# RWKV-7 scan on one core: where the N masks, the 16-row substitution and its buffers stand

## The chip, the cores and the metric

One core of one Trainium2 chip runs one program. The time is that of the device, in microseconds, for the whole program. The profile is one execution of it, with the instructions of TensorE (PE), its weight loads (PEld), VectorE (DVE), ScalarE (ACT), GpSimd (POOL) and the DMA issues of SyncE (SP).

## The reference, cut to what matters

Two transformer blocks are computed for 1024 tokens of width 1024 in float32. The first has two mixers side by side, an RWKV-7 mixer and a gated linear attention, and a feed-forward part; the second has neighbourhood attention, a convolution and a multilayer perceptron. The change touches the RWKV-7 scan alone, which has 8 heads of 64 channels and runs once forward and once backward:

```
def step(S, inp):
    r_t, w_t, k_t, v_t, kk_t, b_t = inp
    sa = jnp.einsum('bhij,bhj->bhi', S, -kk_t)
    S = (S * w_t[:, :, None, :] + sa[..., None] * b_t[:, :, None, :]
         + v_t[..., None] * k_t[:, :, None, :])
    return S, jnp.einsum('bhij,bhj->bhi', S, r_t)
y = (rwkv7_scan(r_h, heads(decay[:, :, 0]), k_h, v_h, kk, b_h, False)
     + rwkv7_scan(r_h, heads(decay[:, :, 1]), k_h, v_h, kk, b_h, True))
```

Everything ahead of the scan makes r, k, v, kk, b and the decays; what follows normalises y, multiplies by a gate and projects.

## The kernel before

Each engine has its own program, written out by hand in `rwkv_scan_pe`, `rwkv_scan_dve`, `rwkv_scan_act`, `rwkv_scan_pool` and `rwkv_scan_sp`. Engines meet through counters: `.then_inc(*dve.one("nm", n, d))` marks a point, and `wait_ge(dve["nm", n, d])` waits for it. An engine does its instructions in the order in which they are written, so that a wait holds all that stands behind it. `dve.c` makes VectorE wait for its own last instruction first.

The scan is done in 16 chunks (`NSUB`) of 64 tokens. The 16 pairs of head and direction lie as 8 lanes, 4 for each direction `d`, with two heads one above the other in the 128 partitions. Inside a chunk the recurrence is a triangular system, whose matrix has to be inverted. For a chunk n the steps are:

- `products(n)`, VectorE, lines 1697 to 1702: the factor F, four wide multiplies that make AR (three homes) and BK (one home), and a copy of the last decay. It waits for the exponentials, for the outputs of chunk n-3, and for the transposes of chunk n-1 (`pe["tr", n - 1, 1]`), which read BK.
- TensorE, gram products `gb` and `gk` (line 1480, names s_AR and s_BK): the products of BK with AR, in PSUM. VectorE multiplies them by the triangular masks at line 1716: `gb` gives NM (the N masks, counter `nm`), `gk` gives MM (the M masks, counter `mm`).
- TensorE, transposes of BK (line 1555, counter `tr`), which write to the same PSUM bank as `gb` and so wait for `nm`. ScalarE copies them out as BKT (line 1623).
- The diagonal 16x16 blocks of NM go by DMA to DRAM (line 1446) and come back as 16 small loads (line 1423) onto 32 partitions in `N16`: ten issued by SyncE, six by GpSimd. GpSimd writes the identity to `Z16` (line 1638), and `substitute_dve` inverts the blocks there in 15 steps of two dependent small instructions (lines 1662 and 1663), with a transposed copy at the end (line 1665, counter `x16`).
- The inverse goes to DRAM (line 1455) and back in 8 loads (line 1432, `inverse_back`) into ZZ, four by SyncE and four by GpSimd.
- Two levels join the 16-row blocks to 32 and to 64 rows: TensorE `p4`, VectorE mask `t4` (line 1736), TensorE `l4` (lines 1578, 1579), VectorE `zz` (line 1740), then `p5`, `t5` (line 1744), `l5`, and `xt` (line 1750), which gives XT, the whole inverse.
- With the state: right sides `rh`, ScalarE Rn, TensorE `uu` with XT, ScalarE U, TensorE `ss`, VectorE state sum (line 1711) and scaling by F (line 1721), TensorE outputs `yy`, taken to B by ScalarE in the first half (line 1619) and added there by VectorE in the second (line 1727).

The loop runs over u from -2 to 15. A pass u works on three chunks at once: the state of chunk u, the levels of chunk m = u + 1, and the masks and the substitution of chunk n = u + 2; it also makes the products of chunk u + 3. TensorE's order in a pass is: gb, gk (n), uu, ss, yy (u), tr (n), in every second pass the sums of the log decays (line 1489), rh (m), p4, l4, p5, l5 (m). VectorE's order is: state sum (u), N and M masks (n), state scaling, output sums (u, second half), products (u + 3), t4, zz, t5 (m), substitution steps 0 to 3 (n), xt (m), substitution steps 4 to 14 and the copy (n). gb of a pass waits for t5 and gk for xt of the pass before. In pass 14 four multiplies for a later stage (line 1910) stand ahead of t4.

SyncE's order per chunk n (`rwkv_scan_sp`) is: wait for the N masks of n, N out; wait for the inverse of n - 1 to be in DRAM, its four loads; wait for N to be out, ten block loads; in every second chunk the load of the decays (line 1441); wait for `x16` of n, inverse out. N out and the block loads count on one counter, `t_n`. GpSimd's order is: inverse loads of n - 1, identity of n, block loads of n.

Of the kernel before, what the change touches and what calls it, by code (L numbers as in the profile page):

```python
# [10 lines left out]
ALU = mybir.AluOpType  # L11
ACTF = mybir.ActivationFunctionType
# [13 lines left out]
NSUB = 16  # L26
# [150 lines left out]
def rep(ap, n):  # L177
    return ap.unsqueeze(1).to_broadcast([ap.shape[0], n] + list(ap.shape[1:]))
# [29 lines left out]
class Kernel:  # L208
    def __init__(self, nc, ins, out):
# [12 lines left out]
        self.t_lat = [self.transfer(f"t_lat{k}") for k in range(2)]  # L222
        self.t_zb, self.t_nb = self.transfer("t_zb"), self.transfer("t_nb")
        self.t_x = [self.transfer(f"t_x{k}") for k in range(3)]
        self.t_a = [self.transfer(f"t_a{k}") for k in range(4)]
# [99 lines left out]
    def plan_block1(self):  # L325
# [76 lines left out]
        self.En, self.Eb = sb("s_En", [PART, LANES, 2, CH]), sb("s_Eb", [PART, LANES, 2, CH + 1])  # L402
        self.eye16, self.N16 = sb("eye16", [32, 2, 16, 16]), sb("s_N16", [32, 2, 16, 16])
        self.XT, self.S = ([sb(n, [PART, LANES, CH]) for k in range(2)] for n in ("s_XT", "s_S"))
# [1013 lines left out]
    def blocks_there(self, eng, counter, n, ks):  # L1418

        nd = self.dram["nd"]  # L1420
        for k in ks:
            for d in range(2):
                eng.e.dma_start(self.N16[4 * k:4 * k + 4, d], nd[n % 2, 4 * d:4 * d + 4, 16 * k:16 * k + 16, 16 * (k % 4):16 * (k % 4) + 16]) \
                    .then_inc(*counter.one("in", n))
# [10 lines left out]
    def rwkv_scan_sp(self):  # L1435
        sp, sg, pe, dve = self.sp, self.dram["sg"], self.pe, self.dve
        nd, zd = self.dram["nd"], self.dram["zd"]

        def sig(t):
            sp.wait_ge(pe["cum", t - 1, 1])  # L1440
            sp.e.dma_start(self.sig[:], sg[:, t].rearrange("d p c -> p d c")).then_inc(*self.t_in.one("sig", t))

        sig(1)
        for n in range(NSUB):
            sp.wait_ge(dve["nm", n, 1])
            sp.e.dma_start(nd[n % 2].rearrange("l p c -> p l c"), self.NM[n % 3][:, :, 0, :]).then_inc(*self.t_n.one("out", n))
            if n:
                sp.wait_ge(self.t_z["out", n - 1], self.pool["zero"])
                self.inverse_back(sp, self.t_z, n - 1, range(0, 8, 2))
            sp.wait_ge(self.t_n["out", n])  # L1450
            self.blocks_there(sp, self.t_n, n, range(0, 5))
            if n % 2 and (n + 3) // 2 < NBLK:
                sig((n + 3) // 2)
            sp.wait_ge(dve["x16", n])
            sp.e.dma_start(zd[n % 2].rearrange("k x d w i c -> (k x) (d w i c)"), self.Z16[:].rearrange("p d w i c -> p (d w i c)")) \
                .then_inc(*self.t_z.one("out", n))
        sp.wait_ge(self.t_z["out", NSUB - 1])
        self.inverse_back(sp, self.t_z, NSUB - 1, range(0, 8, 2))
        i = self.i
        sp.wait_ge(dve["pr", NSUB - 1])  # L1460
        for dst, src in ((self.r_hones[:], i["k_head_ones"]), (self.r_hsel2[:], i["k_head_sel"]), (self.r_gup[:], i["rwkv_g_up"][0]),
                         (self.r_sglo2[:], self.dram["lo"][2])):
            sp.e.dma_start(dst, src).then_inc(*self.t_misc.one("ro"))
        sp.e.dma_start(self.r_v[:], self.dram["v"]).then_inc(*self.t_keep.one("v_back"))
        self.meet(sp, "rwkv_scan", self.t_misc["ro"], self.t_keep["v_back"])
# [138 lines left out]
    def rwkv_scan_act(self):  # L1604
        pe, act, dve, ps = self.pe, self.act, self.dve, self.ps
        L = [slice(0, 4), slice(4, 8)]
        for u in range(-2, NSUB):
# [12 lines left out]
            if u + 2 < NSUB:  # L1620
                for d in range(2):
                    act.wait_ge(pe["tr", u + 2, d])
                    act.e.activation(self.BKT[(u + 2) % 3][:, L[d]].rearrange("p l w c -> p l (w c)"), self.fb(d, 0), ACTF.Copy) \
                        .then_inc(*act.one("BKT", u + 2, d))
            if u % 2 == 0 and (u + 4) // 2 < NBLK:
                self.exps_act((u + 4) // 2)
        self.meet(act, "rwkv_scan")

    def rwkv_scan_pool(self):
        pool = self.pool  # L1630
        pool.e.memset(self.S[0][:], 0.0).then_inc(*pool.one("zero"))
        for n in range(NSUB + 1):
            if n:
                pool.wait_ge(self.t_z["out", n - 1], pool["zero"])
                self.inverse_back(pool, self.t_zb, n - 1, range(1, 8, 2))
            if n < NSUB:
                pool.wait_ge(self.t_misc["r_const"])
                pool.e.tensor_copy(self.Z16[:, :, 1], self.eye16[:]).then_inc(*pool.one("one", n))
                pool.wait_ge(self.t_n["out", n])
                self.blocks_there(pool, self.t_nb, n, range(5, 8))  # L1640
        self.meet(self.pool, "rwkv_scan")

    def substitute_dve(self, n, first, end):
# [3 lines left out]
        if first == 0:  # L1647
            dve.wait_ge(self.pool["one", n])
            dve.wait_ge(self.t_n["in", n], self.t_nb["in", n])
        N, Z = self.N16[:, 0], self.Z16[:, 0, 1]  # L1650

# [15 lines left out]
    def rwkv_scan_dve(self):  # L1667
# [11 lines left out]
        def products(n):  # L1679
# [22 lines left out]
            dve.c.tensor_copy(lanes(self.last[:]), end).then_inc(*dve.one("pr", n))  # L1702

        products(0)
        for u in range(-2, NSUB):
            n, m = u + 2, u + 1
# [5 lines left out]
            if n < NSUB:  # L1712
                for w, to, name in ((0, self.NM[n % 3], "nm"), (1, self.MM[n % 3], "mm")):
                    for d in range(2):
                        dve.wait_ge(pe[("gb", "gk")[w], n, d])
                        dve.e.tensor_tensor(to[:, L[d]].rearrange("p l a b -> p l (a b)"), self.fb(d, w),
                                            rep(self.gram_mask[:, d].rearrange("p a b -> p (a b)"), 4), ALU.mult).then_inc(*dve.one(name, n, d))
            if u >= 0 and m < NSUB:
# [12 lines left out]
            if u + 3 < NSUB:  # L1731
                products(u + 3)
            if 0 <= m < NSUB:
                for d in range(2):
                    dve.wait_ge(pe["p4", m, d])
                    dve.e.tensor_tensor(self.T[:, L[d]], self.hb(d, 0), rep(self.lev_mask[:, 0, d], 4), ALU.mult).then_inc(*dve.one("t4", m, d))
            if 0 <= m < NSUB:
                for d in range(2):
# [6 lines left out]
            if n < NSUB:  # L1745
                self.substitute_dve(n, 0, 4)
            if 0 <= m < NSUB:
                for d in range(2):
                    dve.wait_ge(pe["l5", m, d])
                    dve.e.tensor_tensor(self.XT[m % 2][:, L[d]], self.ZZ2[:, L[d], 1], self.hb(d, 1), ALU.subtract).then_inc(*dve.one("xt", m, d))  # L1750
            if n < NSUB:
                self.substitute_dve(n, 4, 15)
        self.meet(dve, "rwkv_scan")
# [1488 lines left out]
```

## Time and profile before

| what | us |
|---|---|
| three runs: lowest, median, highest | 3499.68, 3499.96, 3500.47 |
| the profiled execution's own time | 3487.46 |
| its span | 3486.2 |
| the scan, from its first product on VectorE to its last inverse, in the span | 700 to 1076 |

Over the whole span TensorE is busy for 3188.2 us (91%), VectorE for 2211.3 (63%), ScalarE for 971.9 (28%) and GpSimd for 469.5 (13%). Times in rows are microseconds from the start of the span. A row of a timeline gives the start, the duration, the engine, the line of the program, what is written and read, the shapes and, in brackets, how long the engine had been idle and what ended that.

### The profile page before, as it was taken

What the parts mean: (1) busy time and instruction counts of PE and PEld (TensorE: products, weight loads), DVE (VectorE), ACT (ScalarE), POOL (GpSimd) and SP (SyncE); (2) the same over time, 40 slices, a digit from 0 to 9 for tenths busy, and PEclk for the clock granted to TensorE, in tenths of its full rate; (3) what the DMA queues carried; (4) which work ended last, traced back from release to release, by engine and by line L of the source; (5) the groups of instructions that cost most, each with busy time, mean ns of one, the idle gap of its engine ahead of it and who ended that gap; (6) DMA issues with size and microseconds to landing.
All of it is one profiled execution on the core that took longest, in us unless ns stands there. A gap on an engine that the chain in (4) does not pass through costs nothing.

```text
span 3486.2 us, 58522 instructions
## 1 busy us (share of the span) xinstructions
PE 3188.2 (91%) x25755; PEld 2622.4 (75%) x25755; DVE 2211.3 (63%) x2948; ACT 971.9 (28%) x1514; POOL 469.5 (13%) x373
## 2 busy tenths in 40 slices
PE   6988788979987999999999897998998799999996
PEld 4777767778885878888888676875667688888885
DVE  5758655778887444444444575997556566666666
ACT  4544233312113221111111444112663111111112
POOL 2530023423224000000000121000001011111110
PEclk9979788989998999999999998999999899999999
DMA  4410044322224011111111202114001111111111
GB/s 131 122 66 14 16 142 138 111 45 42 37 36 166 19 55 51 40 55 53 38 55 43 91 31 74 49 43 99 2 2 61 43 49 49 49 49 49 49 49 67
DMA packets 242726, 207.27 MB, mean 59 GB/s; under 512 B 66744, under 2 KB 205255, under 8 KB 241959
## 3 DMA queue, kind: packets, MB, share of 16 engines
q1 hardware_dynamic: 223527, 176.82, 17.1%
q10 hardware_dynamic: 13824, 25.17, 2.2%
q0 software_dynamic: 5120, 1.53, 0.5%
q8 instruction: 202, 3.31, 0.4%
q14 instruction: 53, 0.43, 0.0%
HBM read 171.93 MB, written 29.64 MB: 58 GB/s over the span
## 4 chain that ended last, share of the span: by engine, by line
PE 70%; DVE 17%; ACT 5%; POOL 2%; issue 2%; DMA 2%; SPq 1%; ACTq 0%; DVEq 0%; POOLq 0%
PE ps L2169 23%; PE ps L2184 17%; PE ps L2031 5%; PE ps L636 3%; PE ps L637 3%; PE ps L638 3%; DVE Yc L2794 2%; DVE s_tmp L1662 2%; DVE s_Z L1663 2%; PE ps L2893 2%; PE ps L2921 1%; PE ps L2911 1%; PE ps L1480 1%; POOL a_x L2544 1%; PE ps L1008 1%
## 5 line engine op out<-in xcount | busy, mean ns | idle before, releaser
L3198 DVE TENSOR_TENSOR H<-H,ps 128x1024 f32<-128x1024 f32 x256 | 312.7, 1221 | 181.6 <-PE ps L2184 174.8
L2334 DVE TENSOR_TENSOR fsum<-fsum,ps 128x1024 f32<-128x1024 f32 x168 | 205.2, 1221 | 312.4 <-PE ps L2184 310.3
L2184 PE MATMUL ps<-dh,hh 128*128 128x512 f32 x864 | 340.0, 393 | 19.9 <-DVE hl L2149 13.9
L2184 PE MATMUL ps<-dl,hh 128*128 128x512 f32 x864 | 338.7, 392 | 0.0
L2184 PE MATMUL ps<-dh,hl 128*128 128x512 f32 x864 | 338.6, 392 | 0.0
L2169 PE MATMUL ps<-hn_h,uh 128*128 128x512 f32 x704 | 275.8, 392 | 7.2 <-DVE ul L1779 4.7
L2169 PE MATMUL ps<-hn_l,uh 128*128 128x512 f32 x704 | 275.4, 391 | 0.0
L2169 PE MATMUL ps<-hn_h,ul 128*128 128x512 f32 x704 | 275.3, 391 | 0.0
L2169 PE MATMUL ps<-hx_h,uh 128*128 128x512 f32 x512 | 200.9, 392 | 8.4 <-DVE hx_l L2149 5.3
L2184 PEld LDWEIGHTS ps<-dh,hh 128*128 128x128 f32 x864 | 163.8, 190 | 58.0 <-DVE hl L2149 15.6
L2169 PE MATMUL ps<-hx_l,uh 128*128 128x512 f32 x512 | 200.4, 391 | 0.0
L2169 PE MATMUL ps<-hx_h,ul 128*128 128x512 f32 x512 | 200.4, 391 | 0.0
L2184 PEld LDWEIGHTS ps<-dh,hl 128*128 128x128 f32 x864 | 163.7, 189 | 34.4
L2184 PEld LDWEIGHTS ps<-dl,hh 128*128 128x128 f32 x864 | 163.7, 189 | 33.9
L2544 POOL TENSOR_TENSOR a_x<-a_x,a_t 128x512 f32<-128x512 f32 x84 | 129.0, 1535 | 338.0 <-ACT a_t L2533 335.5
L3168 POOL TENSOR_TENSOR dw<-dw,g_row 128x1024 f32<-128x1024 f32 x32 | 77.7, 2431 | 710.0 <-DMA dw<-in_w_mlp_dram 710.0
L2169 PEld LDWEIGHTS ps<-hn_h,uh 128*128 128x128 f32 x704 | 133.1, 189 | 35.5 <-DVE ul L1779 5.2
L2794 DVE SCALAR_TENSOR_TENSOR Yc<-cp,cols,Yc 128x1024 f32<-128x1024 f32 x120 | 154.2, 1285 | 4.3
L2169 PEld LDWEIGHTS ps<-hn_l,uh 128*128 128x128 f32 x704 | 133.2, 189 | 27.7
L2169 PEld LDWEIGHTS ps<-hn_h,ul 128*128 128x128 f32 x704 | 133.1, 189 | 27.8
L636 PE MATMUL ps<-hx_h,cw 128*128 128x512 f32 x320 | 130.8, 409 | 17.2 <-DVE cw L616 7.5
L3177 ACT ACTIVATE relu<-ps 128x1024 f32<-128x1024 f32 x32 | 32.9, 1029 | 404.9 <-PE ps L2169 404.9
(473 smaller groups left out, 7345.8 us busy)
## 6 DMA issues: line engine op xcount, KB each, us to landing
aw<-in_w_ada_dram ACTq DMA_DIRECT2D x96, 256.0 KB, 2.9
uw<-in_w_mlp_dram SPq DMA_DIRECT2D x32, 512.0 KB, 4.3
dw<-in_w_mlp_dram SPq DMA_DIRECT2D x32, 512.0 KB, 5.2
uw<-in_ffn_gate_dram SPq DMA_DIRECT2D x22, 512.0 KB, 4.0
uw<-in_ffn_up_dram SPq DMA_DIRECT2D x22, 512.0 KB, 5.3
dw<-in_ffn_down_dram SPq DMA_DIRECT2D x22, 512.0 KB, 5.9
cw<-in_w_in_dram SPq DMA_DIRECT2D x20, 512.0 KB, 3.8
o_w<-in_w_out_dram SPq DMA_DIRECT2D x16, 512.0 KB, 9.9
```

The costliest lines, as they stand in the source:

```text
L636: pe.e.matmul(ps[0:m, 2 * (j % 2) + h, :], wh[:, k, :], xh, start=(k == 0), stop=False)
L637: pe.e.matmul(ps[0:m, 2 * (j % 2) + h, :], wh[:, k, :], xl, start=False, stop=False)
L638: mm = pe.e.matmul(ps[0:m, 2 * (j % 2) + h, :], wl[:, k, :], xh, start=False, stop=(k == kc - 1))
L1662: dve.c.tensor_tensor(part, col, pivot, ALU.mult).then_inc(*dve.one())
L2031: mm = pe.e.matmul(self.ps[:, 2 * (t % 2) + hf, :], x[a](k), w[b](k)[:, half(hf)], start=(n == 0 and m == 0), stop=(n == len(order) - 1 an ...
L2169: mm = pe.e.matmul(ps[:, 2 * pair + h, :], w[:, col], x[h][v][:, k, :], start=(k == 0 and m == 0), stop=(k == DC - 1 and m == 2))
L2184: mm = pe.e.matmul(ps[:, 2 * pair + hf, :], v[s][:, blk(t)], w[:, half(hf)], start=(m == 0), stop=(m == 2))
L2334: return dve.c.tensor_tensor(f, f, new, ALU.add) if g else dve.c.tensor_copy(f, new)
L2544: pool.c.tensor_tensor(acc[:], acc[:], self.a_t[who][:], ALU.add).then_inc(*pool.one("ada", q, who))
L2794: dve.c.scalar_tensor_tensor(out=o, in0=x[:, w:w + TOK], scalar=self.col("dw", n + 4 * w), in1=o, op0=ALU.mult, op1=ALU.add) \
L3168: pool.e.tensor_tensor(w, w, self.g2_row[:], ALU.mult).then_inc(*pool.one("m", "dw", g))
L3198: return dve.c.tensor_tensor(h, h, self.ps[:, 4 + 2 * (t % 2):6 + 2 * (t % 2), :], ALU.add)
```

## The change

- The N masks of chunk n + 1 are made in the pass before: in pass u they stand behind `xt` and ahead of substitution step 9. The M masks stay where they were.
- The substitution of chunk n is cut otherwise: steps 0 to 6 stand ahead of the mask `t4`, step 7 behind it, step 8 behind `t5`, steps 9 to 14 behind the N masks of n + 1.
- `N16` has two homes, used in turn.
- SyncE's order per chunk becomes: N out, wait, ten block loads, and then wait for `x16` of the chunk before, inverse out, wait, its four loads. N out has a counter of its own, `t_no`.
- GpSimd does its six block loads ahead of its four inverse loads, and no longer writes the identity; ScalarE does (copy of 32x512), behind BKT of the chunk and once the inverse of the chunk before is in DRAM.

```diff
-        self.eye16, self.N16 = sb("eye16", [32, 2, 16, 16]), sb("s_N16", [32, 2, 16, 16])
+        self.eye16, self.N16 = sb("eye16", [32, 2, 16, 16]), [sb("s_N16", [32, 2, 16, 16]) for k in range(2)]
...
+        def back(n):
+            sp.wait_ge(dve["x16", n])
+            sp.e.dma_start(zd[n % 2].rearrange("k x d w i c -> (k x) (d w i c)"), self.Z16[:].rearrange("p d w i c -> p (d w i c)")) \
+                .then_inc(*self.t_z.one("out", n))
+            sp.wait_ge(self.t_z["out", n], self.pool["zero"])
+            self.inverse_back(sp, self.t_z, n, range(0, 8, 2))
...
         for n in range(NSUB):
             sp.wait_ge(dve["nm", n, 1])
-            sp.e.dma_start(nd[n % 2].rearrange("l p c -> p l c"), self.NM[n % 3][:, :, 0, :]).then_inc(*self.t_n.one("out", n))
+            sp.e.dma_start(nd[n % 2].rearrange("l p c -> p l c"), self.NM[n % 3][:, :, 0, :]).then_inc(*self.t_no.one("out", n))
+            sp.wait_ge(self.t_no["out", n])
+            self.blocks_there(sp, self.t_n, n, range(0, 5))
             if n:
-                sp.wait_ge(self.t_z["out", n - 1], self.pool["zero"])
-                self.inverse_back(sp, self.t_z, n - 1, range(0, 8, 2))
-            sp.wait_ge(self.t_n["out", n])
-            self.blocks_there(sp, self.t_n, n, range(0, 5))
+                back(n - 1)
...
+                act.wait_ge(self.t_z["out", u + 1] if u + 1 >= 0 else self.t_misc["r_const"])
+                act.e.activation(self.Z16[:, :, 1], self.eye16[:], ACTF.Copy).then_inc(*act.one("one", u + 2))
...
         for n in range(NSUB + 1):
+            if n < NSUB:
+                pool.wait_ge(self.t_no["out", n])
+                self.blocks_there(pool, self.t_nb, n, range(5, 8))
             if n:
                 pool.wait_ge(self.t_z["out", n - 1], pool["zero"])
                 self.inverse_back(pool, self.t_zb, n - 1, range(1, 8, 2))
-            if n < NSUB:
-                pool.wait_ge(self.t_misc["r_const"])
-                pool.e.tensor_copy(self.Z16[:, :, 1], self.eye16[:]).then_inc(*pool.one("one", n))
-                pool.wait_ge(self.t_n["out", n])
-                self.blocks_there(pool, self.t_nb, n, range(5, 8))
...
         products(0)
+        masked(0, 0)
...
             if n < NSUB:
-                for w, to, name in ((0, self.NM[n % 3], "nm"), (1, self.MM[n % 3], "mm")):
...
+                masked(1, n)
...
             if u + 3 < NSUB:
                 products(u + 3)
+            if n < NSUB:
+                self.substitute_dve(n, 0, 7)
...
+            if n < NSUB:
+                self.substitute_dve(n, 7, 8)
...
             if n < NSUB:
-                self.substitute_dve(n, 0, 4)
+                self.substitute_dve(n, 8, 9)
...
+            if n + 1 < NSUB:
+                masked(0, n + 1)
             if n < NSUB:
-                self.substitute_dve(n, 4, 15)
+                self.substitute_dve(n, 9, 15)
```

`masked(w, n)` holds the body of the old loop: for each direction it waits for `gb` or `gk` and multiplies by the triangular mask.

## Rows read from the trace of the kernel before

**Rows 1.** Busy time by stretch, in the scan: stretch, length, then each engine, granted clock.
```profile
800.00:900.00 100.00, 91.66 (x2465) 86.26 (x2463) 80.93 (x236) 20.74 (x52) 29.40 (x49) 1.00 0.22 38
1000.00:1060.00 60.00, 50.39 (x1434) 47.28 (x1432) 46.70 (x140) 7.00 (x16) 17.31 (x29) 1.00 0.17 25
```

**Rows 2.** Timeline of VectorE: start of the first level mask in three passes.
```profile
734.49 0.89 DVE L1736 TENSOR_TENSOR s_T<-ps,lev_mask 128x256 f32<-128x256 f32 x2 [0.61 <-PE ps L1480]
...
1048.21 0.89 DVE L1736 TENSOR_TENSOR s_T<-ps,lev_mask 128x256 f32<-128x256 f32 x2 [3.94 <-PE ps L1480]
...
1069.88 0.42 DVE L1736 TENSOR_TENSOR s_T<-ps,lev_mask 128x256 f32<-128x256 f32 x1 [0.56 <-PE ps L1480]
```

**Rows 3.** Chain of waits in one pass: start, duration, engine or DMA, what.
```profile
882.05 0.60 DVE s_Z L1665
...
883.31 1.21 DVE s_NM L1716 x2
884.54 0.38 SPq L1446
...
886.73 3.61 DMA s_ZZ<-zd_dram
```

**Rows 4.** Timeline of VectorE, two steady passes, from one level mask to the next.
```profile
868.39 0.89 DVE L1736 TENSOR_TENSOR s_T<-ps,lev_mask 128x256 f32<-128x256 f32 x2 [1.20 <-PE ps L1480]
870.10 0.69 DVE L1740 TENSOR_TENSOR s_ZZ<-s_ZZ,ps 128x512 f32<-128x512 f32 x1 [0.82 <-PE ps L1579]
...
873.08 0.20 DVE L1662 TENSOR_TENSOR s_tmp<-s_N,s_Z 32x30 f32<-32x30 f32 x1
...
875.00 0.73 DVE L1750 TENSOR_TENSOR s_XT<-s_ZZ,ps 128x256 f32<-128x256 f32 x2
...
877.59 0.28 DVE L1662 TENSOR_TENSOR s_tmp<-s_N,s_Z 32x128 f32<-32x128 f32 x1
...
886.51 0.17 DVE L1697 TENSOR_TENSOR s_F<-s_last,s_Eb 128x8 f32<-128x8 f32 x1
886.60 0.68 DVE L1698 TENSOR_TENSOR s_AR<-r_kk,s_Eb 128x512 f32<-128x512 f32 x1
887.20 1.12 DVE L1699 TENSOR_TENSOR s_BK<-r_bb,s_En 128x512 f32<-128x512 f32 x1
...
891.12 0.89 DVE L1736 TENSOR_TENSOR s_T<-ps,lev_mask 128x256 f32<-128x256 f32 x2 [1.37 <-PE ps L1480]
```

**Rows 5.** Timeline of VectorE, first pass (u = -2): products of chunk 1.
```profile
710.80 0.17 DVE L1697 TENSOR_TENSOR s_F<-s_last,s_Eb 128x8 f32<-128x8 f32 x1 [1.17 <-PE ps L1555]
```

**Rows 6.** Timeline of ScalarE, first pass: the second direction of BKT.
```profile
710.80 0.60 ACT L1623 ACTIVATE s_BKT<-ps 128x512 f32<-128x512 f32 x1 [0.25 <-PE ps L1555]
```

**Rows 7.** Timeline of TensorE, one steady pass: gram products, uu, transposes.
```profile
873.50 3.91 PE L1480 MATMUL ps<-s_AR,s_BK 64*64 64x128 f32 x64
877.25 1.10 PE L1480 MATMUL ps<-s_Rn,s_XT 64*64 64x64 f32 x32
...
883.97 2.08 PE L1555 MATMUL ps<-eye,s_BK 64*64 64x64 f32 x64 [0.56 <-DVE s_NM L1716]
```

**Rows 8.** Waits from 740 to 1040 us: total, times, longest.
```profile
PEld ps L1480 <- DVE s_XT L1750: 3.7, 14, 0.3
```

**Rows 9.** Timeline of GpSimd, the steady pass: the identity's copy.
```profile
887.14 0.62 POOL L1638 COPY s_Z<-eye 32x512 f32<-32x512 f32 x1
```

**Rows 10.** Timeline of SyncE's queue, first passes and second to last.
```profile
707.91 0.38 SPq L1446 DMA_DIRECT2D nd_dram<-s_NM  x1
710.50 3.57 SPq L1423 DMA_DIRECT2D s_N<-nd_dram  x10
726.15 0.32 SPq L1455 DMA_DIRECT2D zd_dram<-s_Z  x1
...
1062.45 0.32 SPq L1455 DMA_DIRECT2D zd_dram<-s_Z  x1
```

**Rows 11.** Timeline of VectorE, pass 14: the four multiplies for the later stage.
```profile
1064.46 4.87 DVE L1910 SCALAR_TENSOR_TENSOR r_rkv<-r_rkv,cols 128x1024 f32<-128x1024 f32 x4
```

More of the change, by code:

```diff
@@ L223, in __init__ @@
         self.t_zb, self.t_nb = self.transfer("t_zb"), self.transfer("t_nb")
+        self.t_no = self.transfer("t_no")
         self.t_x = [self.transfer(f"t_x{k}") for k in range(3)]
@@ L1422, in blocks_there @@
             for d in range(2):
-                eng.e.dma_start(self.N16[4 * k:4 * k + 4, d], nd[n % 2, 4 * d:4 * d + 4, 16 * k:16 * k + 16, 16 * (k % 4):16 * (k % 4) + 16]) \
+                eng.e.dma_start(self.N16[n % 2][4 * k:4 * k + 4, d], nd[n % 2, 4 * d:4 * d + 4, 16 * k:16 * k + 16, 16 * (k % 4):16 * (k % 4) + 16]) \
                     .then_inc(*counter.one("in", n))
@@ L1445, in rwkv_scan_sp @@
             sp.wait_ge(dve["nm", n, 1])
-            sp.e.dma_start(nd[n % 2].rearrange("l p c -> p l c"), self.NM[n % 3][:, :, 0, :]).then_inc(*self.t_n.one("out", n))
+            sp.e.dma_start(nd[n % 2].rearrange("l p c -> p l c"), self.NM[n % 3][:, :, 0, :]).then_inc(*self.t_no.one("out", n))
+            sp.wait_ge(self.t_no["out", n])
+            self.blocks_there(sp, self.t_n, n, range(0, 5))
             if n:
-                sp.wait_ge(self.t_z["out", n - 1], self.pool["zero"])
-                self.inverse_back(sp, self.t_z, n - 1, range(0, 8, 2))
-            sp.wait_ge(self.t_n["out", n])
-            self.blocks_there(sp, self.t_n, n, range(0, 5))
+                back(n - 1)
             if n % 2 and (n + 3) // 2 < NBLK:
                 sig((n + 3) // 2)
[L1454 to L1458, printed above, removed]
+        back(NSUB - 1)
         i = self.i
@@ L1647, in substitute_dve @@
         if first == 0:
-            dve.wait_ge(self.pool["one", n])
+            dve.wait_ge(self.act["one", n])
             dve.wait_ge(self.t_n["in", n], self.t_nb["in", n])
-        N, Z = self.N16[:, 0], self.Z16[:, 0, 1]
+        N, Z = self.N16[n % 2][:, 0], self.Z16[:, 0, 1]
         def both(x, second, first, rest):
@@ L1702, in products, with masked @@
             dve.c.tensor_copy(lanes(self.last[:]), end).then_inc(*dve.one("pr", n))
+        def masked(w, n):
+            to, name = ((self.NM[n % 3], "nm"), (self.MM[n % 3], "mm"))[w]
+            for d in range(2):
+                dve.wait_ge(pe[("gb", "gk")[w], n, d])
+                dve.e.tensor_tensor(to[:, L[d]].rearrange("p l a b -> p l (a b)"), self.fb(d, w),
+                                    rep(self.gram_mask[:, d].rearrange("p a b -> p (a b)"), 4), ALU.mult).then_inc(*dve.one(name, n, d))
         products(0)
+        masked(0, 0)
         for u in range(-2, NSUB):
@@ L1712, in rwkv_scan_dve @@
             if n < NSUB:
-                for w, to, name in ((0, self.NM[n % 3], "nm"), (1, self.MM[n % 3], "mm")):
[L1714 to L1717, printed above, removed]
+                masked(1, n)
             if u >= 0 and m < NSUB:
```

## The prediction

> **What bounds the kernel now.** I read the stretches first. In the RWKV scan neither engine is full all the time: in the middle of it TensorE is busy for 91.7 of 100 us and VectorE for 80.9, at a granted clock of 1.00, the upper of its two levels [rows 1]. So the scan is bound by a chain that goes round once per pass (one pass per chunk of 64 tokens, 16 chunks). The start of the first level mask of each pass gives the beat: from 734.49 to 1048.21 us there are 14 passes, 313.7 us, 22.4 us each [rows 2].
>
> The chain of waits shows the round: the substitution and its copy end on VectorE, VectorE does the state sum and the N masks, SyncE's queue (held by its wait for the N masks) only then issues the return of the inverse blocks, they land 3.6 us after the last issue, TensorE multiplies, and VectorE masks the level [rows 3]. VectorE stood idle 1.37 us ahead of that mask [rows 4]. That idle time is what a substitution begun earlier could fill.
>
> What the reader must see beside it is a second chain, hidden today. The line that starts the products of chunk u+3 waits for the transposes of chunk u+2, as they read the one BK buffer that the products overwrite. In the first pass that wait is bare: F begins at 710.80, after 1.17 us idle put down to the transposes (L1555), at the moment at which ScalarE begins to read the last of them [rows 5, 6]. In a steady pass the wait is covered: the transposes start at 883.97 and take some 2.05 us, so end at 886.0, and F begins at 886.51 [rows 4, 7].
>
> **The steady pass, worked out.** I call L the start of the gram products of the next chunk; TensorE does its work in a fixed order from there. In the pass shown L is 873.50 [rows 7]. From L to the end of the transposes TensorE has the gram products (3.9 us), the inverse's product, state, outputs and transposes: 886.0 - 873.5 = 12.5 us. Two waits in it go: the 0.56 us of the transposes for the N mask (the passes looked at have 0.55 or 0.56) [rows 7], because that mask is now made a pass earlier; and up to 0.3 us of the second gram product for XT (3.7 us in 14 passes, 0.26 each) [rows 8], because XT has two substitution steps ahead of it where it had four. So the transposes end at L + 11.7.
>
> VectorE meanwhile: XT to L + 0.9; the N masks, two, together 1.2 us [rows 3], the second not before the gram product of its direction is through, at about half of 3.9 us: end at L + 2.7; steps 9 to 14 of the substitution, from step 7's start at 877.59 to the copy at 882.05, 4.46 us, less two steps of 0.63: 3.2 us [rows 3, 4], so L + 5.9. Copy, state sum, M masks and state scaling take today, with the N masks between them, 882.05 to 886.51; less the N masks' 1.2 that is 3.3 us: L + 9.2. In the second half of the scan the output sums follow, which TensorE allows at about L + 9.6 (the transposes' 883.97 less their wait, and less 0.26): L + 10. The products can't start there, since the transposes end at L + 11.7. **So VectorE idles 1.5 to 2.5 us there**, where today it does not; the idle time has moved, not gone.
>
> After it come, in VectorE's own order, products and then seven substitution steps, all ahead of the level mask. Products: today from F at 886.51 to the mask at 891.12 less its idle 1.37, 3.2 us, in which one of the four wide multiplies took 1.12 us, beside GpSimd's copy of the identity from 887.14 on; another of them took 0.68 us [rows 4, 9]. That copy leaves GpSimd, so I take 3.2 less 0.4, 2.8 us (bounds 2.8 and 3.2). Seven steps: the first four 1.98 us (873.08 to the XT pair at 875.00 and on it by 0.06 us), the next three from that pair's end at 875.76 to 877.59, 1.83 us [rows 4]. With 0.15 us of hand-over the mask starts at L + 11.7 + 2.8 + 1.98 + 1.83 + 0.15 = L + 18.5.
>
> From the mask to the next L: 868.39 to 873.50, 5.1 us, all of it TensorE and VectorE in turns [rows 4, 7]. Step 7 (0.63 us) fits in the 0.82 us idle that VectorE has behind the masks, and step 8 stands behind the last mask where four steps stood. Nothing is won or lost there (bounds -0.1 and +0.3). The pass is 5.1 + 18.5 = **23.6 us against 22.4**, and in the 13 passes that have products +15.6 us.
>
> **The identity on ScalarE.** The trace has no such copy on ScalarE. From below it costs nothing; from above, ScalarE's 128x512 evacuation takes 0.60 us [rows 6], and at that price it ends at L + 12.9, behind the evacuation of the transposes (it waits for the inverse of the chunk before to have left Z16, too, at L + 11.6 with N's 2.6 us), 1.6 us ahead of the first step at L + 14.5. I take nothing; queued behind it are exponentials and right sides not needed before that. The Trainium skill (SBUF — State Buffer, "Who interferes with whom") says that only VectorE and GpSimd share a port pair, and that ScalarE has its own. The stretched multiply agrees for GpSimd, and no run here yet shows the identity written from ScalarE. By the rule the products take 2.8 us; were the stretch to move along to ScalarE, 3.2 us, and the sum 5.2 us more.
>
> **The queues.** SyncE now does per chunk: N out, wait, ten block loads into the other home, and only then the inverse out and back. N out to the first block load took 2.6 us (707.91 to 710.50), the ten loads 3.6 us [rows 10], so that the inverse leaves at L + 2.7 + 0.1 + 2.6 + 3.6 = L + 9.0, though it is ready at L + 6.5. From its issue to the mask there were 7.4 us where no N load stood between (1062.45 to 1069.88) [rows 2, 10], so the mask could start at L + 16.4. In a crowded queue, with 2.6 us to land as for N and then the chain's 6.2 us from the end of N's issue (884.54 + 0.38) to the mask at 891.12 [rows 3, 4], it is L + 17.8. Both are ahead of L + 18.5, so the delay is hidden, with 0.7 to 2.1 us to spare. The same cover takes GpSimd's six loads and the sigma load, and the second home, without which the loads would have to wait for the substitution. The first step's other inputs (blocks at L + 11, identity) are there as well.
>
> **The ends of the scan.** First pass: chunk 0's inverse leaves today at 726.15, behind the copy of 0.6 us and steps 9 to 14 of 3.2 [rows 10]. Now the N mask of chunk 1 stands before step 9, at about 722.4 to 723.7; N lands at 726.3, the ten loads end at 729.9, the inverse leaves at 730.0, 3.8 us later. With the 7.4 to 8.8 us from there to the mask (as above), it comes at about 738.1 instead of 734.49: +3.6 us (bounds +1.2, the mask's own time, and +5). Second to last pass: no products are left, the mask comes at L + 17.1 against L + 17.5: -0.4 us. Last: today 1048.21 to 1069.88, 21.7 us [rows 2]. Now XT ends 6.0 us behind the mask (5.1 + 0.9), with nine steps done and not four; steps 9 to 14 and the copy take 3.8, and no N and no loads are ahead of the inverse, so it leaves at +9.9 and would allow the mask at +17.3. VectorE has the last output sum before it, which TensorE allows at +12.2 (from the inverse's product at 877.25 to the end of the outputs at 883.4 are 6.2 us [rows 7]), and four bonus products, 4.87 us [rows 11]: +17.5. So some -4.1 us (bounds -5 and -2).
>
> **Sum:** +15.6 + 3.6 - 0.4 - 4.1 = +14.7 us. The profiled execution took 3487.5 us over a span of 3486.2, so it would become 3502.2; the median of the runs shown, 3499.96, lies 12.5 us above the profiled one, and the same difference on it gives **3515 us**. The rest of the kernel is untouched.
>
> **Rivals.**
> (a) Not slower: the transposes are not the last thing the products wait for. It decides if they end before L + 9.2. Then the mask waits for the inverse alone, at L + 16.4 to 17.8: a pass of 21.5 to 22.9, and with the ends -13 to +6 us, near 3496 us, within the measurement's reach of no change or a little under it. For it speaks the idle VectorE today; against it that TensorE's work up to there is 11.7 us without a wait. In the full form of it the inverse comes free of the queue too and TensorE alone sets the pass: 11.7, 1 us of the sums (they run in every second pass), 2 of right sides and 0.7 to the mask, so 20.5 us, -25 us, 3476 us.
> (b) The inverse comes later than the mask could start, as ten loads stand ahead of it and N lands in crowded queues. At 1 us beyond L + 18.5 it adds 13 us: 3528 us. For it speak the 3.6 us from the last issue to the landing [rows 3], behind only four returns and one N; against it the 0.7 to 2.1 us to spare.
> (c) The clock. A pass with longer idle stretches on TensorE might be granted less than 1.00. Busy 84% of the time (50.4 of 60 us) it still had 1.00 [rows 1]; the new pass has 91.7% x 22.4 / 23.6 = 87% in the middle. As an estimate, half the clock doubles TensorE's 20 us of a pass, so that one pass at it would cost some +20 us. The rows speak against it.
>
> **Chances.** Forecast 0.77; (a) 0.06 near no change and 0.05 in full; (b) 0.08; (c) 0.02; unseen, of either sign, 0.02. The range takes the forecast's own bounds (steady passes +11 to +21, start and end -2 to +3) and half of (b): 3505 to 3526. I take 0.2%, 7 us, as what can be told from no change: slower 0.85, same 0.09, faster 0.06.
>
> **What the profile after would show.** Right: pass 23.6 us from level mask to level mask; VectorE idle ahead of F, put down to L1555's transposes, 1.5 to 2.5 us a pass; no idle worth a name ahead of the level mask; transposes without a wait for the N mask; all four wide multiplies at 0.68; the inverse leaving 2 us or more behind its copy. Wrong: an idle ahead of the level mask that ends with TensorE behind a transfer (b), F following the scaling without a gap (a), or a granted clock under 1.00 in the middle of the scan (c).

## The result and the profile after

The changed kernel takes 3526.45 us in the median of 4 runs (3520.85 to 3528.37); the kernel before, run with it, 3499.82 us (3496.81 to 3500.47). The ratio is 1.0075, with a 95% interval of 1.0058 to 1.0093: **slower by 26.6 us**, with 20 to 33 us by the interval, where 15 were forecast. The range ended at 3526, half a microsecond short of the median. The profiled execution took 3520.85 us over a span of 3519.5, 33.4 us more than the one of before. That is more than the medians differ by, as the profiled execution of before was 12.4 us under its median and this one 5.6.

First the stretches of the scan, as in [rows 1]: stretch, length, busy time of each engine, then granted clock, DMA share and GB/s.

```profile
800.00:900.00 100.00, 87.00 (x2295) 83.97 (x2293) 74.66 (x224) 20.64 (x50) 24.55 (x41) 0.93 0.23 40
900.00:1000.00 100.00, 86.95 (x2226) 84.22 (x2224) 74.43 (x217) 18.22 (x44) 24.08 (x40) 0.90 0.21 37
```

TensorE is busy for 87% of the time, which is the very share that the prediction gave, but at a clock of 0.93 and 0.90, not 1.00. Next VectorE's timeline, the lines that answer to [rows 2] and [rows 4]: F (now line 1700) and the first level mask (now line 1745).

```profile
764.58 0.73 DVE L1745 TENSOR_TENSOR s_T<-ps,lev_mask 128x256 f32<-128x256 f32 x2
...
781.42 0.17 DVE L1700 TENSOR_TENSOR s_F<-s_last,s_Eb 128x8 f32<-128x8 f32 x1 [2.69 <-PE ps L1558]
781.51 0.68 DVE L1701 TENSOR_TENSOR s_AR<-r_kk,s_Eb 128x512 f32<-128x512 f32 x1
782.12 0.68 DVE L1702 TENSOR_TENSOR s_BK<-r_bb,s_En 128x512 f32<-128x512 f32 x1
...
790.00 0.42 DVE L1745 TENSOR_TENSOR s_T<-ps,lev_mask 128x256 f32<-128x256 f32 x1 [1.84 <-PE ps L1483]
...
808.38 0.17 DVE L1700 TENSOR_TENSOR s_F<-s_last,s_Eb 128x8 f32<-128x8 f32 x1 [2.55 <-PE ps L1558]
...
815.04 0.74 DVE L1745 TENSOR_TENSOR s_T<-ps,lev_mask 128x256 f32<-128x256 f32 x2
...
831.89 0.17 DVE L1700 TENSOR_TENSOR s_F<-s_last,s_Eb 128x8 f32<-128x8 f32 x1 [2.69 <-PE ps L1558]
...
838.56 0.73 DVE L1745 TENSOR_TENSOR s_T<-ps,lev_mask 128x256 f32<-128x256 f32 x2
```

The reader is to see three things. F waits for the transposes (line 1558), 2.5 to 2.7 us idle in each pass of the first half and 1.45 to 1.6 in the second, about as foreseen. From F to the mask it is 6.66 us (808.38 to 815.04) with nothing in between to wait for, except once, at 790.00, where the inverse came late. And from a mask to the next F it is 16.84 us (764.58 to 781.42) in one pass and 18.38 us (790.00 to 808.38) in the next, for the same instructions. The view of the waits gives the idle time ahead of F from 760 us on (total, times, longest):

```profile
DVE s_F L1700 <- PE ps L1558: 26.0, 12, 2.7
```

Where the 1.5 us come from stands in short stretches of one such pass:

```profile
781.00:784.00 3.00, 2.06 (x69) 1.92 (x63) 2.58 (x5) 1.75 (x4) 1.15 (x3) 1.00 0.08 8
784.00:787.00 3.00, 0.00 (x0) 0.00 (x0) 2.49 (x13) 0.00 (x0) 1.09 (x2) 1.00 0.68 111
787.00:790.00 3.00, 1.15 (x22) 1.18 (x24) 1.06 (x4) 0.00 (x0) 0.00 (x0) 0.60 0.28 105
790.00:793.00 3.00, 3.00 (x62) 3.00 (x60) 1.81 (x5) 0.00 (x0) 0.00 (x0) 0.50 0.02 5
793.00:796.00 3.00, 2.81 (x72) 2.68 (x69) 1.53 (x4) 0.00 (x0) 0.00 (x0) 0.76 0.00 0
796.00:799.00 3.00, 2.94 (x66) 2.80 (x62) 2.38 (x7) 0.00 (x0) 0.00 (x0) 1.00 0.02 5
```

TensorE stands idle, the clock goes to 0.50, the lower of its two levels, and the level's products that follow run at it, and there the pass is made of TensorE and VectorE in turns. TensorE's own timeline has the idle time ahead of the product with the inverse (s_ZZ,s_NM) and behind it, ahead of the level's product (line 1581). The first row is of the kernel before; the 5.79 us are the pass above, the last two rows the pass from 833:

```profile
867.67 1.15 PE L1480 MATMUL ps<-s_ZZ,s_NM 64*64 64x64 f32 x32 [1.96 <-DMA s_ZZ<-zd_dram]
...
788.85 1.97 PE L1483 MATMUL ps<-s_ZZ,s_NM 64*64 64x64 f32 x32 [5.79 <-issue]
...
836.23 1.97 PE L1483 MATMUL ps<-s_ZZ,s_NM 64*64 64x64 f32 x32 [2.71 <-issue]
839.01 0.49 PE L1581 MATMUL ps<-s_T,s_ZZ 64*64 64x64 f32 x4 [0.81 <-DVE s_T L1745]
```

The same product took 1.15 us before; here it takes 1.97. Over the scan the two profiled executions compare as follows, from the starts of the first F (700.20 and 704.07) and of the level masks.

| stretch | before | after | difference | forecast |
|---|---|---|---|---|
| start of the span to the first F | 700.20 | 704.07 | +3.9 | 0 |
| first F to first level mask | 34.3 | 35.8 | +1.5 | +3.6 |
| 13 passes | 291.1 | 321.5 | +30.4 | +15.6 |
| second to last pass | 22.6 | 23.6 | +1.0 | -0.4 |
| last pass | 21.7 | 17.9 | -3.8 | -4.1 |
| last mask to the end | 2416.3 | 2416.7 | +0.3 | 0 |

### The profile page after: what moved, and what is told of

Read it like the earlier page. It is cut to its first block, busy times and chain, and to the rows that moved or that the text cites. A ratio compares the mean times of both kernels' runs of the same rounds, so it can differ in the third digit from the quotient of the medians.

```text
span 3519.5 us, 58525 instructions
## 1 busy us (share of the span) xinstructions
PE 3207.3 (91%) x25755; PEld 2646.9 (75%) x25755; DVE 2207.6 (63%) x2948; ACT 978.8 (28%) x1530; POOL 459.5 (13%) x357
## 3 DMA queue, kind: packets, MB, share of 16 engines
q1 hardware_dynamic: 223527, 176.82, 16.8%
## 4 chain that ended last, share of the span: by engine, by line
PE 73%; DVE 14%; ACT 5%; POOL 2%; DMA 2%; issue 2%; SPq 1%; ACTq 0%; DVEq 0%; POOLq 0%
PE ps L2182 23%; PE ps L2197 17%; PE ps L2044 5%; PE ps L1483 4%; PE ps L637 3%; PE ps L638 3%; PE ps L639 3%; DVE Yc L2807 2%; PE ps L2906 2%; PE ps L2934 1%; PE ps L2924 1%; POOL a_x L2557 1%; PE ps L1009 1%; DVE s_tmp L1665 1%; DVE s_Z L1666 1%
## 5 line engine op out<-in xcount | busy, mean ns | idle before, releaser
L2197 PE MATMUL ps<-dh,hh 128*128 128x512 f32 x864 | 340.1, 394 | 19.9 <-DVE hl L2162 13.9
L2197 PEld LDWEIGHTS ps<-dh,hh 128*128 128x128 f32 x864 | 163.8, 190 | 58.0 <-DVE hl L2162 15.6
L2182 PEld LDWEIGHTS ps<-hn_l,uh 128*128 128x128 f32 x704 | 133.2, 189 | 27.7
```

The costliest lines, as they stand in the source:

```text
L2182: mm = pe.e.matmul(ps[:, 2 * pair + h, :], w[:, col], x[h][v][:, k, :], start=(k == 0 and m == 0), stop=(k == DC - 1 and m == 2))
L2197: mm = pe.e.matmul(ps[:, 2 * pair + hf, :], v[s][:, blk(t)], w[:, half(hf)], start=(m == 0), stop=(m == 2))
```

## The experiments

Theory A: the change makes VectorE wait for the transposes and puts seven steps behind them (the forecast's 23.5 us a pass), and what is above that is TensorE's clock, which falls as TensorE is left idle in one piece. Theory B: what is above it is the inverse, which comes late through the queues. Theory C: the seven steps alone are what costs. All ratios are to the kernel before, run beside each group on the same chip; its own medians there were 3493.7 to 3496.4 us, so that medians of different groups are compared only to some 3 us. All kernels but the control are the changed one with the edits named. "Extra products 12 / 4 / 6" are 12 ahead of the product with the inverse in passes with odd u, 4 in those with even u, and 6 behind it.

| run | us, median | ratio, 95% interval | 13 passes, us each |
|---|---|---|---|
| the changed kernel again | 3524.78 | 1.0094 (1.0078 to 1.0109) | 24.8 |
| extra products 12 / 4 / 6 | 3519.98 | 1.0080 (1.0063 to 1.0098) | 24.3 |
| extra products 10 / 3 / 2 | 3510.21 | 1.0036 (1.0024 to 1.0047) | 23.6 |
| before, with extra products | 3497.29 | 1.0000 (0.9990 to 1.0009) | 23.0 |
| decays loaded early | 3529.31 | 1.0081 (1.0060 to 1.0101) | 25.1 |
| inverse ahead of six loads | 3520.93 | 1.0065 (1.0051 to 1.0079) | 24.6 |
| transposes early | 3504.48 | 1.0025 (1.0009 to 1.0041) | 23.5 |
| cut as before | 3516.72 | 1.0070 (1.0048 to 1.0093) | 24.1 |
| transposes early, both queues | 3486.25 | 0.9970 (0.9958 to 0.9983) | 22.1 |
| the same, with extra products | 3490.11 | 0.9982 (0.9969 to 0.9995) | 22.3 |

The last column is one profiled execution each, from the first level mask to the fourteenth, divided by 13; it was 22.4 before and 24.7 in the changed kernel's first profile.

**The changed kernel again.** No edit.

> The changed kernel as it is, as the anchor. Both theories: 3520 to 3529 us, 0.6 to 0.8% over the kernel before. Theory A (the clock): passes of 23.5 us where the granted clock stays at 1.00, 24.5 to 27 us where it falls after TensorE's wait for the inverse; from the level mask to F 16.85 us in the first kind, 18 us or more in the second, and from F to the level mask 6.67 us in nearly all. Theory B (the inverse comes late, by itself): the time between F and the level mask would vary instead.

Three passes lasted 23.5 us, with 16.8 us from mask to F, and the others 24.6 to 26.7, with 17.9 to 18.8 us from mask to F. From F to the mask it was 6.67 us in eleven of 13, and 8.40 and 7.74 us in two, where the inverse came late. So A holds for most of it and B for about 3 us.

**Idle TensorE filled.** `spare_pe(k)` issues k products of the 128x128 triangular matrices (`tri`, there for the sums of the log decays) into a bank that the level's products overwrite, once the M masks have been taken from it.

```diff
+                if n < NSUB:
+                    pe.wait_ge(dve["mm", n, 0], dve["mm", n, 1])
+                    self.spare_pe(12 if u % 2 else 4)
                 pe.wait_ge(self.t_z["in", m], self.t_zb["in", m])
...
+                if n < NSUB:
+                    self.spare_pe(6)
                 for d in range(2):
                     pe.wait_ge(dve["t4", m, d])
```

> The changed kernel with idle TensorE filled: 12 (odd passes) or 4 (even passes) extra 128x128 products into a bank nobody reads ahead of the product with the inverse, and 6 behind it. They compute nothing that is used. Theory A (the part above 23.5 us a pass is the clock): granted clock 0.99 or more in the middle of the scan, every pass from mask to F 16.85 us, 10 to 15 us less than the changed kernel, near +12 us on the kernel before. Theory B (the excess is transfers and queues, the clock only follows): no gain, within 3 us of the changed kernel, or slower by the extra products, up to 2 us a pass.

The clock came back to 1.00 from the fourth pass on, and the even passes with it to 16.7 us from mask to F. The odd passes did not get there: 17.3 to 18.3 us, at a clock of 1.00, with TensorE busy for nearly all of the pass, as the second of these two stretches (an even and an odd pass) shows:

```profile
844.00:867.67 23.67, 22.14 (x566) 21.12 (x565) 18.11 (x55) 6.12 (x15) 5.96 (x10) 1.00 0.18 29
867.67:892.63 24.96, 24.63 (x605) 23.77 (x601) 18.17 (x53) 3.89 (x9) 5.94 (x10) 1.00 0.26 48
```

The six products behind, which are 12 rows of the trace, stood in front of the level's own: these begin at 869.56, 1.89 us behind the start of the mask, where it is 0.46 us in the changed kernel (815.04 to 815.50).

```profile
868.03 1.60 PE L1514 MATMUL ps<-tri 128*128 128x128 f32 x12
869.56 0.34 PE L1591 MATMUL ps<-s_T,s_ZZ 64*64 64x64 f32 x4
```

The gain was 5 us where 10 to 15 were expected, too little to tell A from B. So the next run had 10, 3 and 2 of them.

> The changed kernel with fewer extra TensorE products than in the run with 12, 4 and 6 of them: 10 (odd passes) or 3 (even) ahead of the product with the inverse, 2 behind it. Theory A (the clock): the even passes stay at 16.7 us from mask to F, the odd ones fall from 17.3-18.3 to about 17 us, as fewer extra products stand ahead of the level's own; granted clock 0.98 or more in the middle; mean pass 23.6 to 24.0 us, 7 to 13 us under the changed kernel. Theory B (the transfers, not the clock): no less than 3 us under the changed kernel.

```profile
838.85:862.24 23.39, 22.69 (x573) 21.45 (x571) 18.06 (x54) 5.99 (x15) 5.96 (x10) 1.00 0.20 31
862.24:885.76 23.52, 21.70 (x568) 20.96 (x568) 18.05 (x55) 4.00 (x9) 5.95 (x10) 1.00 0.23 48
885.76:909.13 23.37, 22.18 (x569) 21.06 (x569) 18.04 (x54) 5.99 (x15) 5.94 (x10) 1.00 0.20 32
```

Each stretch is a pass from mask to mask. From the second on all are 23.3 to 23.6 us, the 13 together 306.7 us; the forecast had 306.8. That the two agree to 0.1 us is in part luck: the first pass still lost 1.9 us at a clock of 0.94, and the other twelve average 23.44 and not 23.6. Nothing but extra work on TensorE (and its wait for the M masks) was added, and some 15 us went away, 14.6 by the medians and 16.0 in the 13 passes. All but the late inverse of the excess over the forecast is the clock.

**Control.** The kernel before, with four such products ahead of the product with the inverse in odd passes.

```diff
+                    self.spare_pe(4 if u % 2 else 0)
```

> Control: the kernel before, with 4 extra TensorE products ahead of the product with the inverse in the odd passes, where TensorE waits up to 2 us. Its granted clock in the scan is 1.00 already. Theory A (the extra products pay by holding the clock alone): nothing to gain, within 3 us of the kernel before, passes 22.1 to 22.7 us. If extra products gain 5 us or more here too, they act in another way than through the clock.

A ratio of 1.0000: in a kernel that loses the clock little or not at all, extra products bring nothing. Its profiled execution had longer passes than expected, 22.3 to 24.3 us. Two were long by a late inverse (the mask waited 3.12 and 1.83 us), one by late N blocks, for which the substitution's first step waited 1.41 us, and in one the clock fell to 0.93 here too, right behind the mask that had waited 3.12 us. The 13 passes took 299.1 us, 8 more than in the profiled execution of before, at a time near the median. So that one was a fast one of its kernel, and how the 26.6 us of the medians divide among the stretches isn't shown, only how the 33.4 us of the profiles do.

**Decays loaded early.** The 512 KB load no longer stands right behind the return of the inverse.

```diff
         for n in range(NSUB):
+            if n % 2 and (n + 3) // 2 < NBLK:
+                sig((n + 3) // 2)
             sp.wait_ge(dve["nm", n, 1])
```

> The changed kernel with the 512 KB load of the decays issued ahead of the wait for the N masks and no longer right behind the inverse's return. Theory B (that load delays the inverse in the odd passes, and TensorE's wait there grows from 3 to 5.8 us): TensorE's wait ahead of the product with the inverse 2 us or less in odd passes, no idle ahead of the level mask, the clock falls less, 5 to 12 us under the changed kernel. Theory A alone (the wait for the transposes and the seven steps make TensorE idle in any case, 2 us each pass ahead of the level's products): the clock still falls in most passes, 0 to 4 us under it.

TensorE's waits ahead of the product with the inverse came to 26.3 us in 13 passes, against 27.7 in the changed kernel; the longest was 3.33 us and no longer 5.79, but those of the odd passes did not come down to the 2 us of the expectation. In the pass below it waited 1.85 us ahead of that product and 2.50 us behind it, and the clock fell in every pass:

```profile
841.70 1.15 PE L1483 MATMUL ps<-s_ZZ,s_NM 64*64 64x64 f32 x32 [1.85 <-DMA s_ZZ<-zd_dram]
845.35 0.48 PE L1581 MATMUL ps<-s_T,s_ZZ 64*64 64x64 f32 x4 [2.50 <-DVE s_T L1745]
```

No gain, so that load is not the cause.

**The inverse ahead of six loads.**

```diff
+            self.blocks_there(sp, self.t_n, n, range(0, 2))
+            if n:
+                out(n - 1)
+            self.blocks_there(sp, self.t_n, n, range(2, 5))
```

> The changed kernel with the inverse sent out by SyncE ahead of six of its ten block loads. Forecast's term (the delay of the inverse in the queue is hidden behind VectorE's work): from mask to mask nothing changes where the clock stays, 23.5 us; TensorE's idle time only moves from ahead of the product with the inverse to behind it. Theory A: 0 to 4 us under the changed kernel. Theory B (late inverse starves TensorE and so brings the clock down): 5 us or more under it.

From F to the mask 6.67 us in all passes; the inverse was never late. The idle time moved behind the product with the inverse, 1.5 to 4.5 us there, and the clock fell in 11 of 13 passes. The 13 took 319.7 us, against 321.5 and 322.7 in the two profiles of the changed kernel; the median is 3.9 us under the repeated run. The ratio is 1.0065 against 1.0094 and 1.0075, which would be 3 to 10 us, and the groups of runs don't tell these apart. So the delay in the queue is hidden for the most part, as the prediction's queue part says, and it isn't the late inverse alone that brings the clock down: the wait for the mask does as well.

```profile
838.39 1.15 PE L1489 MATMUL ps<-s_ZZ,s_NM 64*64 64x64 f32 x32 [1.72 <-DMA s_ZZ<-zd_dram]
842.16 0.48 PE L1587 MATMUL ps<-s_T,s_ZZ 64*64 64x64 f32 x4 [2.63 <-DVE s_T L1751]
```

**Transposes early.** This takes away what VectorE waits for: TensorE does the transposes ahead of the outputs, ScalarE its BKT first, and the only multiply that needs the outputs is done last.

```diff
+            if n < NSUB:   # transposes, tr(n), moved up as they are
             if u >= 0:     # outputs, yy(u)
...
-            if n >= 3:
-                dve.wait_ge(pe["yy", n - 3, 1])
             if n:
                 dve.wait_ge(pe["tr", n - 1, 1])
...
+            if n >= 3:
+                dve.wait_ge(pe["yy", n - 3, 1])
+            dve.e.tensor_tensor(lanes(AR[:, :, 1]), ...)
...
             if u + 3 < NSUB:
                 products(u + 3)
+            # output sums of the second half, moved down as they are
```

> The changed kernel with the transposes ahead of the outputs on TensorE, ScalarE's BKT and identity ahead of its copy of the outputs, and on VectorE the r multiply last of the products and the output sums behind them. Theory A (the forecast's step: the products wait for the transposes): VectorE's idle time ahead of F falls from 2.6 to under 0.7 us, the level mask waits for the inverse instead, passes of 21.5 to 23 us, and if TensorE's waits shorten the clock holds: 3490 to 3502 us, 25 us or more under the changed kernel. Theory C (seven substitution steps ahead of the mask are what costs, whatever stands ahead of them): passes stay at 23.5 us or more.

```profile
779.58 0.75 DVE L1729 TENSOR_TENSOR s_S<-s_S,s_F 128x256 f32<-128x256 f32 x2
780.47 0.17 DVE L1699 TENSOR_TENSOR s_F<-s_last,s_Eb 128x8 f32<-128x8 f32 x1
...
782.83 0.69 DVE L1705 TENSOR_TENSOR s_AR<-r_rkv,s_Eb 128x512 f32<-128x512 f32 x1 [0.38 <-PE ps L1483]
...
791.54 0.42 DVE L1746 TENSOR_TENSOR s_T<-ps,lev_mask 128x256 f32<-128x256 f32 x1 [2.99 <-PE ps L1483]
```

F follows the state's scaling with no idle time, and from mask to F it is 14.3 us where the clock holds, 2.5 us less than 16.85. The best pass took 21.46 us with the same seven steps, so C is out. Then the inverse is what comes last (2.99 us here), and part of the gain is lost to it, and to the clock, which was 0.90 to 0.95 in nine of 13 passes: 20 us under the changed kernel, where 25 or more were expected, and still above the one before.

**Cut as before.**

```diff
-                self.substitute_dve(n, 0, 7)     # ahead of t4
-                self.substitute_dve(n, 7, 8)     # behind t4
-                self.substitute_dve(n, 8, 9)     # behind t5
+                self.substitute_dve(n, 0, 4)     # behind t5
...
                 masked(0, n + 1)
-                self.substitute_dve(n, 9, 15)
+                self.substitute_dve(n, 4, 15)
```

> The changed kernel with the substitution cut as in the kernel before (nothing ahead of the level masks, steps 0 to 3 behind t5, 4 to 14 behind the N masks). Theory A: the seven steps, 3.85 us, leave the way from F to the mask, but XT and the inverse come later, so the mask waits for the inverse: VectorE idle 2 to 4 us ahead of it, passes 23 to 24.5 us, no gain of 3.85 us a pass. Theory C: passes shorten by 3 us or more, to 20.5 us.

```profile
884.10 0.89 DVE L1743 TENSOR_TENSOR s_T<-ps,lev_mask 128x256 f32<-128x256 f32 x2 [2.33 <-PE ps L1483]
...
903.62 0.17 DVE L1700 TENSOR_TENSOR s_F<-s_last,s_Eb 128x8 f32<-128x8 f32 x1
908.30 0.89 DVE L1743 TENSOR_TENSOR s_T<-ps,lev_mask 128x256 f32<-128x256 f32 x2 [1.90 <-PE ps L1483]
```

Passes of 23.0 to 25.1 us, with 1.3 to 4.2 us idle ahead of the mask: the seven steps are gone from there and the inverse stands in their place, as A has it. The clock was 0.91 to 0.95 in six of them.

**Transposes early, with both queue edits.**

> The run with the transposes ahead of the outputs, and with both queue changes (decays loaded early, the inverse sent ahead of six block loads). If in the run with the early transposes alone the inverse's return is what is left (VectorE idle 1 to 3 us ahead of the level mask in half of its passes, 23.4 us a pass), passes become 21.5 to 22.3 us, with the clock at 0.97 or more, 12 us or more under it, and 0 to 8 us under the kernel before. If VectorE's own work is what is left, passes stay at 23 us or more, within 4 us of it.

```profile
784.62:806.05 21.43, 20.64 (x560) 20.04 (x560) 18.13 (x55) 6.11 (x15) 5.95 (x10) 1.00 0.28 54
827.48:851.32 23.84, 22.27 (x560) 21.53 (x560) 18.14 (x55) 6.11 (x15) 5.97 (x10) 0.93 0.27 51
938.91:960.99 22.08, 18.86 (x544) 18.20 (x544) 18.79 (x57) 3.36 (x7) 5.96 (x10) 1.00 0.20 31
```

This version beats both kernels: 0.3% under the one before, its interval clear of 1 (9 us by the medians, where up to 8 were expected), and 38 us under the repeated run of the changed one. Most passes are at 21.4 us (first half) or 22.1 us (second); in the second stretch above the clock fell once more, and it did in two others.

**The same, with extra products** (6, 2 and 1).

> The run with the transposes ahead of the outputs and both queue changes, with 6 (odd passes) or 2 (even) extra products ahead of the product with the inverse and 1 behind. There three passes of 13 lost 0.6 to 2.4 us at a granted clock of 0.93 to 0.96. Theory A: those come back to 21.4 (first half) and 22.1 us (second), 3 to 6 us less than without, 10 to 16 us under the kernel before. Otherwise the extra products stand in the way: equal or slower.

From the second pass on the clock was at 1.00 and the even passes lost nothing to it, but all of the first half took 21.7 to 22.0 us and not 21.4, as extra products stood ahead of the level's own. The first and the tenth to the eleventh pass were long in this execution too. The second expectation came true: no gain, 3490.11 us against 3486.25.

## Why the prediction was wrong

The direction was right and the size too small: +26.6 us instead of +15. **The step that failed is rival (c), "The clock", to which it gave 0.02**: "Busy 84% of the time [...] it still had 1.00 [...]; the new pass has [...] 87% [...]. [...] The rows speak against it." The sum so had the clock at nothing. The share of busy time over a pass was the wrong reading. The share came out at the 87% foreseen and the clock at 0.93 and 0.90, and even that 87% is luck, as the low clock lengthened TensorE's busy time, from 20.4 to 21.2 us a pass, together with the pass. Nor does the share decide in other rows: a pass with 18.86 of 22.08 us busy (85%) kept 1.00 (the run with both queue edits, at 938.91), and one with 23.37 of 25.41 (92%) had 0.87 (the changed kernel, at 886.86). What the extra products took away was idle time in one stretch.

Before, the longest wait of TensorE in a steady pass was some 2 us. The change put 2.1 to 5.8 us ahead of the product with the inverse in the passes without sums of the decays, and 0.8 to 2.3 us behind it in most passes, ahead of the level's product. The prediction named "longer idle stretches" and had what it needed to size them: by its own times TensorE ends the right sides at L + 13.7 (11.7 and 2) where no sums stand between, the inverse allows the mask at L + 16.4 to 17.8, so the product with it some 0.7 us ahead of that, and the mask comes at L + 18.5. That is an estimate of 2.0 to 3.4 us idle ahead of the product, and it never put those waits side by side. Its price was that of a whole pass ("some +20 us"); in fact the clock was low for some 3 to 7 us at a time and cost 1.1 to 1.9 us each, in ten of 13 passes, 13.9 us in all. With 1.9 us of the one late inverse and 13 x 23.5 - 291.1 = 14.4 us of the change itself that is the +30.4 us measured between the two profiled executions, to 0.2.

The other steps, one by one:

- The second chain (products behind the transposes) was shown by the bare wait in each pass and by the run that took it away, in which from mask to F went from 16.85 to 14.3 us. The idle time was 2.6 us in the first half and 1.5 in the second (forecast 1.5 to 2.5).
- The pass: 5.1 + 11.7 = 16.8 us from mask to F, measured 16.85; F to mask 6.75, measured 6.67. With the clock held in all but the first, 13 passes took 306.7 us against 306.8.
- Identity on ScalarE: all four wide multiplies take 0.68 us in every pass, and GpSimd does no copy there, so the products take 2.8 us. The rule of the Trainium skill cited for it (SBUF — State Buffer, "Who interferes with whom") agrees with these rows. "I take nothing" for the copy held in the steady passes alone. It stands behind ScalarE's copies of BKT, and VectorE waited for it 1.03 us ahead of chunk 1's substitution and 2.58 us in the second to last pass, where no products stand before the first step:

```profile
1081.19 0.20 DVE L1665 TENSOR_TENSOR s_tmp<-s_N,s_Z 32x30 f32<-32x30 f32 x1 [2.58 <-ACT s_Z L1629]
```

- The queues: the inverse was hidden in 12 of 13 passes of the changed kernel's first profile, and late by 1.84 us in one. Rival (b) was thus worth 2 to 3 us. The prediction allowed the inverse 2.6 us to land in DRAM; behind the block loads it was 2.0 to 3.7 us from its issue to that of its return, and 3.7 in the pass in which it came late (778.86 to 782.59):

```profile
774.94 3.56 SPq L1424 DMA_DIRECT2D s_N<-nd_dram  x10
778.86 0.32 SPq L1446 DMA_DIRECT2D zd_dram<-s_Z  x1
782.59 1.78 SPq L1433 DMA_DIRECT2D s_ZZ<-zd_dram  x4
```

- The ends: the first mask +1.5 and +3.2 us in two executions (forecast +3.6), the last pass -3.8 and -2.2 (forecast -4.1). The second to last was +1.0 at a clock of 0.87, where -0.4 was forecast; with the clock held it was 21.6 us against 22.6.
- 3.9 of the 33.4 us between the two profiled executions lie ahead of the scan, where the instructions are the same. Such a stretch moves from one execution to the next; the repeated run had 704.91 us there, and the control, whose instructions are those of before up to there, 703.90.
- The range: "+11 to +21", "-2 to +3" and half of (b), 6.5 us, taken as they stand on the median of 3500, add up to some 3509 to 3530 us, and not to the 3505 to 3526 that were stated. The measured 3526.45 would lie inside that, and the step that failed is the same.

The sum without the clock, +15, is near what the run with 10, 3 and 2 extra products shows: 3510.2 against 3495.5 us, +14.7 (8 to 16 by its interval). The exact match is luck, as 1.9 us of a lost clock are still in it.

## What to carry to other kernels

When a change gives an engine idle time, ask where that time lies and not only how much of it there is: list TensorE's waits of one pass one after the other, and look at the granted clock in stretches of a few us behind each. When a step is moved to fill an idle engine, look for the waits that are covered today on the instructions around it (here one wait, 0.5 us from showing); the cure was to move what is waited for, the transposes, and not the work that waits. Extra products on TensorE are a cheap test for a lost clock, and a control on a kernel that has lost little or none tells whether they act in another way.

## What the runs showed of the hardware

- TensorE's clock fell within an idle stretch of 2.71 us between 833.5 and 836.2 us (0.81 on average from 834.0 to 836.2, 0.50 from 836.2 to 839.0), and was back at 1.00 from 843 us on. The Trainium skill (TensorE: Matmul & The Clock Gate, Part 1) says that the gate goes by how busy the engine has been recently; the trace agrees in that the fall comes within idle time, and adds that a busy share of 87% over 100 us did not keep the clock here.

```profile
834.00:836.20 2.20, 0.00 (x0) 0.00 (x1) 1.86 (x8) 0.00 (x0) 0.00 (x0) 0.81 0.88 161
836.20:839.00 2.80, 1.97 (x32) 1.81 (x32) 2.53 (x11) 0.00 (x0) 0.00 (x0) 0.50 0.20 78
839.00:843.00 4.00, 3.98 (x80) 3.87 (x80) 1.94 (x5) 0.00 (x0) 0.00 (x0) 0.60 0.02 4
843.00:847.00 4.00, 3.62 (x85) 3.47 (x86) 2.95 (x8) 0.00 (x0) 0.00 (x0) 1.00 0.01 4
...
886.86:912.27 25.41, 23.37 (x560) 22.66 (x560) 18.12 (x54) 6.00 (x15) 6.09 (x10) 0.87 0.17 26
```

- A low clock raises the busy share: in the pass from 886.86 us, the last row above, TensorE was busy for 23.4 of 25.4 us, for the work that took it 21.5 of 22.7 us before (from 868.39 us), at 1.00. The share hides what it should show.
- Open: which length or pattern of idle time decides. In the changed kernel's first profile, passes with 3.20 us ahead of the product with the inverse and 1.15 behind it, or 2.71 and 0.81, lost the clock, those with 1.00 and 1.03, or 1.16 and 0.87, did not, but one with 0.21 and 1.82 did. Of two with no wait ahead of the product, one with 2.08 us behind it kept the clock and one with 2.18 lost it, so these two lengths alone don't decide.
